# Eight modulation products moved from the recurrent input to layer 1's MLP norm

## The reference, cut to what matters

```
ml = silu(c) @ w_mod[i] + b_mod[i]        # six parts of 1024, for each layer i
mc = silu(c_ctx) @ w_mod[i] + b_mod[i]
hl = modulate(rmsnorm(xl, g_pre_mix[i]), ml[0], ml[1])
xl_new = xl + ml[2] * rmsnorm(y_l, g_post_mix[i])
h2 = modulate(rmsnorm(xl_new, g_pre_mlp[i]), ml[3], ml[4])
xl_new = xl_new + ml[5] * rmsnorm(sqrelu_mlp(h2, ...), g_post_mlp[i])
```

## Time and profile before

| | us |
|---|---|
| median of 3 runs | 1718.69 |
| profiled execution | 1716.11 |
| its span | 1714.3 |
| TensorE busy | 1612.4 (94%) |
| VectorE busy | 1153.9 (67%) |
| ScalarE busy | 552.9 (32%) |
| GpSimd busy | 337.2 (20%) |

### The profile page before, as it was taken

How to read it: one execution, slowest core, us unless ns; L and a number is a source line. 1 busy time by engine, 2 the same in 40 slices (tenths; PEclk the granted TensorE clock), 3 DMA queues, 4 the chain that set the end, 5 groups by cost and what they waited for, 6 DMA issues and landing times.

```text
span 1714.3 us, 26801 instructions
## 1 busy us (share of the span) xinstructions
PE 1612.4 (94%) x10898; PEld 1409.1 (82%) x10898; DVE 1153.9 (67%) x1649; ACT 552.9 (32%) x1111; POOL 337.2 (20%) x300
## 2 busy tenths in 40 slices
PE   7998889999999999999888999999999988889997
PEld 6887779998888999987546588888888874779997
DVE  6855777777687788769764574444444788577776
ACT  5434141112724122153575430202022465541112
POOL 1100333332032333300000121111111100133331
PEclk9999999999999999999999999999999998999999
DMA  7733655556755555532101532222222231224551
GB/s 299 260 121 125 254 213 174 184 183 229 262 183 201 181 184 184 189 147 104 52 1 50 203 117 87 97 100 86 98 98 87 74 136 37 79 102 172 185 185 51
DMA packets 69940, 247.54 MB, mean 144 GB/s; under 512 B 7504, under 2 KB 10576, under 8 KB 69712
## 3 DMA queue, kind: packets, MB, share of 16 engines
q1 hardware_dynamic: 69840, 246.18, 40.5%
HBM read 245.10 MB, written 1.05 MB: 144 GB/s over the span
## 4 chain that ended last, share of the span: by engine, by line
PE 71%; DVE 15%; issue 8%; ACT 5%; DMA 1%; POOL 0%; SPq 0%; DVEq 0%; ACTq 0%; POOLq 0%
PE psum L373 19%; PE psum L375 19%; PE psum L374 19%; DVE lo_ring L334 4%; PE psum L1120 2%; PE psum L388 1%; PE psum L390 1%; PE psum L389 1%; DVE c_soft L2152 1%; ACT c_p L1939 1%; DVE relu L1388 1%; PE psum L488 1%; DVE c_conf L2046 1%; DVE c_p L2160 1%; DVE hid_lo L1389 1%
## 5 line engine op out<-in xcount | busy, mean ns | idle before, releaser
L2321 POOL TENSOR_SCALAR hi_ring<-raw_ring 128x1024 fp32r<-128x1024 f32 x296 | 337.0, 1140 | 1355.5 <-PE psum L375 963.5
L334 DVE TENSOR_TENSOR lo_ring<-raw_ring,hi_ring 128x1024 fp32r<-128x1024 f32 x348 | 507.2, 1459 | 51.3 <-PE psum L375 20.9
L373 PE MATMUL psum<-x_hi,hi_ring 128*128 128x256 f32 (+1 forms) x1464 | 460.9, 315 | 16.3 <-DVE x_lo L879 10.5
L374 PE MATMUL psum<-x_lo,hi_ring 128*128 128x256 f32 (+1 forms) x1464 | 456.1, 312 | 0.0
L375 PE MATMUL psum<-x_hi,lo_ring 128*128 128x256 f32 (+1 forms) x1464 | 456.0, 311 | 0.0
L373 PEld LDWEIGHTS psum<-x_hi,hi_ring 128*128 128x128 f32 x1464 | 281.0, 192 | 38.8 <-issue 16.9
L373 PE MATMUL psum<-hid_hi,hi_ring 128*128 128x256 f32 (+1 forms) x992 | 304.8, 307 | 6.4 <-DVE hid_lo L1389 6.4
L375 PE MATMUL psum<-hid_hi,lo_ring 128*128 128x256 f32 (+1 forms) x992 | 302.9, 305 | 0.0
L374 PE MATMUL psum<-hid_lo,hi_ring 128*128 128x256 f32 (+1 forms) x992 | 302.3, 305 | 0.0
L374 PEld LDWEIGHTS psum<-x_lo,hi_ring 128*128 128x128 f32 x1464 | 281.1, 192 | 14.9 <-issue 0.2
L375 PEld LDWEIGHTS psum<-x_hi,lo_ring 128*128 128x128 f32 x1464 | 281.0, 192 | 14.7
(11 more groups left out here) (424 smaller groups left out, 1996.1 us busy)
## 6 DMA issues: line engine op xcount, KB each, us to landing
raw_ring<-weights SPq DMA_DIRECT2D x460, 512.0 KB, 3.2
h_const<-hyb_consts SPq DMA_DIRECT2D x1, 1088.0 KB, 11.1
x<-xT SPq DMA_DIRECT2D x1, 1024.0 KB, 7.5
x<-ctxT SPq DMA_DIRECT2D x1, 1024.0 KB, 16.3
outT<-x SPq DMA_DIRECT2D x4, 256.0 KB, 2.5
shared<-shared_consts SPq DMA_DIRECT2D x1, 398.0 KB, 13.0
par<-params SPq DMA_DIRECT2D x1, 301.5 KB, 7.6
```

Source lines behind the costliest of these rows:

```text
L334: nc.vector.tensor_tensor(lo_ring[:, s, :], raw_ring[:, UNIT_AT[u] % RAW_SLOTS, :], hi_ring[:, s, :].bitcast(F32), ALU.subtract).then_inc( ...
L373: nc.tensor.matmul(bank(u % BANKS, T), w_hi, hi[:, k, 0:T], start=(k == 0), stop=False)
L374: nc.tensor.matmul(bank(u % BANKS, T), w_hi, lo[:, k, 0:T], start=False, stop=False)
L2321: nc.gpsimd.tensor_scalar(hi_ring[:, n % SPLIT_SLOTS, :], raw_ring[:, slot, :], 1.0, 0.0, ALU.mult, ALU.add).then_inc(hi_ready, 1)
```

## The change

The eight products of the recurrent input go; those of the gates stay. All later products thereby stand eight items of `w_mod` earlier in their order, and the last eight get a new place, "gate_mlp", in layer 1 between the two sums of squares. In the stream they stand behind the MLP's first three units. The batches are cut anew, six instead of five; the last one is copied out by ScalarE behind layer 1's squares, turned by TensorE after the first quarter of layer 1's MLP, and taken by VectorE in the second, with the sixth coefficient part alone; the other five parts are worked out in layer 0's MLP as before.

```diff
-REC_MODS = {j: 3 if j == 2 else 1 for j in range(REC_FIRST - 1, KT)}
+REC_MODS = {j: 0 for j in range(REC_FIRST - 1, KT)}
...
-_STREAM += [MLP_UNITS - LEAD, ("mean3", 2), EARLY, ("pre_mix", 7), L2_UNITS - EARLY - MLP_UNITS + LEAD, ("post_mix", 8), ("post_sum", 6), MLP_UNITS - LEAD, L2_UNITS]
+_STREAM += [MLP_UNITS - LEAD, ("mean3", 2), EARLY, ("pre_mix", 7), L2_UNITS - EARLY - MLP_UNITS + LEAD, ("post_mix", 8), ("post_sum", 6), MLP_UNITS - LEAD, L2_UNITS - MLP_UNITS + LEAD, ("gate_mlp", 8), MLP_UNITS - LEAD]
...
-BATCHES = [10, 10, 14, 7, 7]
+BATCHES = [10, 10, 10, 7, 7, 4]
...
-    SUMS_TAKEN = [0, 2, 4, 5]
+    SUMS_TAKEN = [0, 2, 4, 5, 6]
...
-        if late:
-            turn_batch(pe, 4)
+        if m > 1:
+            turn_batch(pe, m + 2)
...
                 take_sums(dve, 2)
-                coef_dve(dve, link, 1)
+                coef_dve(dve, link, 1, 0, 5)
+            if m == 3 and i == 1:
+                take_sums(dve, 3)
+                coef_dve(dve, link, 1, 5)
...
-                squares_act(act, L.norm + 2, L.T, x, "x_updated", L.updated)
+                squares_act(act, L.norm + 2, L.T, x, "x_updated", L.updated, "gate_mlp" if L.l else None)
...
-                if L.l == 0:
-                    mods(pe, "post_mix")
+                mods(pe, "gate_mlp" if L.l else "post_mix")
```

## The result

The kernel after takes 1726.03 us (median of 20 runs, 1719.79 to 1736.31), the kernel before on the same chip 1720.81 (20 runs, 1717.72 to 1725.52): ratio 1.0032 [1.0023, 1.004]. The forecast was 1718.8 with a range of 1714.0 to 1723.0: the time lies outside. The profiled execution of after is its fastest run, 1719.79 us with a span of 1718.0, 3.7 us longer than the 1714.3 of before.

What follows compares the result with a forecast made beforehand. TensorE was suspected, with VectorE and ScalarE next limiting the recurrent stage. Recurrent +0.2 and layer 1 -1.1 + 0.2 + 0.4 + 0.4 made 0.1 us more: median 1718.8 us, range 1714.0 to 1723.0.

Steps and rivals of the forecast that it cites:

- Small parts: Layer 1's row copy, extra turning, coefficient steps and the new batch cut: 0.4 us for the turning, nothing for the rest.
- D: Rival, chance 0.03: the change doesn't do what it says, for instance a batch waits for its rows; a few tenths of us.
- VectorE and ScalarE take over in the recurrent stage: Recurrent stage: gate 2 waits for ScalarE's read behind VectorE's last taps; 1.2 us of 5.2 gained, new idle 3.7 us.
- Rival A: Chance 0.09: TensorE carries the recurrent stage after all and the whole 5.2 us is won, 1713.4 us.
- The clock behind the idle: Recurrent stage: TensorE's clock falls after the new idle before gate 2, costing 1.4 us, so the stage ends 0.2 later.
- rival B: Chance 0.24: VectorE and ScalarE take over as said, but the clock does not fall in front of gate 2; 1717.4 us.
- Layer 1's norm: Post-mix norm: products fill TensorE's 3.04 us idle at full clock, 1.1 us gained, less 0.2 (weights) and 0.4 (GpSimd).
- late weights: Layer 1's post-mix norm: the last product's weights arrive at 1505.7, so the sums end at 1509.8; 0.2 us taken.
- The collision with GpSimd: Layer 1: the fourth MLP unit's hi half on GpSimd runs beside VectorE's gating and slows it; 0.4 us, bounds 0 and 0.85.
- rival C: Chance 0.16: layer 1's products go on the path, their last weights landing 2 us later; +2.3 us, 1721.0.
- The copy of the rows: Layer 1: ScalarE's copy of the product rows, 0.42 us, is hidden before the rstd's wait for the sums: nothing.
- The turning: Layer 1's MLP: one more turning on TensorE, 0.51 us busy, some overlapping the next matmul; 0.4 us more.

Runs made afterwards that it cites:

- E10: Kernel before with the region of y and the hidden tiles 192 bytes later (hid at distance 0, as in after), no product moved: 1724.46 us, ratio 1.0032.
- E11: Kernel after, unedited, run again on the same chip: 1722.79 us, ratio 1.0022 against the kernel before.
- E1: Kernel after with y and the hidden tiles put back at their old addresses (distance 64): 1718.78 us, ratio 1.0004 against the kernel before.
- E8: Kernel after with x and hid both at distance 192: 1713.61 us, ratio 0.9966 against the kernel before.
- E12: Kernel after with x at distance 64, hid at 0 for 512 columns and 192 for 256: 1704.64 us, ratio 0.9932 against the kernel before.
- E5: Kernel before with x and hid both at distance 192, lam's place moved in front of x_hi: 1709.35 us, ratio 0.9945.
- E9: Kernel before with x at distance 64, hid at 0 for 512 columns and at 192 for 256: 1707.54 us, ratio 0.9935.
- E6: Kernel before with x at distance 32 and hid at 96, a single run: 1728.02 us.
- E3: Kernel before with everything 64 bytes further, weights too, so all distances kept: 1717.47 us, ratio 0.999.
- E4: Kernel before with x_hi and what follows moved 64 bytes, y and hid 64 more (x at distance 64, hid at 192): 1710.59 us, ratio 0.9948.
- E2: Kernel before with y and the hidden tiles 64 bytes further (hid at distance 128): 1724.23 us, ratio 1.0028.
- E7: Kernel before with x at distance 160 and hid at 224, a single run: 1730.7 us.

## Why the prediction was wrong

**The step that failed** is the last sentence of "Small parts": "The new cut of the batches (10, 10, 10, 7, 7, 4) ends each batch at the place where it ended before, at most 20 columns instead of 28: nothing." I priced the cut by what it computes. It also sizes two tiles, these push hid_hi by 320 bytes, and the 2304 matmuls of 256 columns on it each lose 0.0022 us, while the 672 of 512 columns gain 0.0023: +3.5 us by the rows (+3.9 with the last 192), +3.3 to +7.7 by E10's interval. No rival had it either; D looked for the batches' side effects in waits. Of the 7.2 us above the forecast 2.1 are the kernel before itself, whose median is 1720.81 over 20 runs and was 1718.69 over the first 3.

**VectorE and ScalarE take over in the recurrent stage: right.** Gate 2 waits for ScalarE's r_i, the idle is 3.44 us (forecast 3.7), 1.08 us is won (forecast 1.2). Rival A, the whole 5.2 us, is refuted by those rows.

**The clock behind the idle: right in direction, too cheap.** I took 1.4 us. It fell in four of five executions and then cost 1.4 to 2.6 (5.03 to 6.19 against 3.60); in the profiled execution of after it cost nothing, which is rival B. The Trainium skill ("TensorE: Matmul & The Clock Gate", "Part 1: The HAM clock gate") has half rate as the resting state; these four agree, at 0.56 in E11's stretch. From the end of the first units to the start of the output units the stage takes 63.83 us before and 62.76 after, 1.1 less; in E1, E11, E8 and E12 it takes 64.22, 65.31, 64.24 and 64.50, against 63.83, 63.92, 63.19 and 63.99 in the kernels with the products in place (before, E10, E5, E9), so 0.4 to 1.4 more. The forecast was 0.2 more.

**Layer 1's norm: right in sum, not in its parts.** Forecast -1.1 + 0.2 + 0.4 = -0.5; measured -0.69, with the clock at 1.00 as expected. The -1.1 shrank to -0.7 since the sums ended 0.88 us behind the last square (1512.48), where I took 0.45 for the four matmuls left. Of the 0.2 for late weights nothing shows. The collision with GpSimd, the 0.4 in it, had no occasion: the weights of that unit came later than I took, and its hi half ran when VectorE's gating was nearly done:

```profile
1511.61 1.05 POOL L2324 TENSOR_SCALAR hi_ring<-raw_ring 128x1024 fp32r<-128x1024 f32 x1 [8.80 <-DMA raw_ring<-weights]
```

VectorE's last gating instruction ran from 1511.03 to 1511.72, in 0.69 us like the others. The products ended at 1508.58, 3.59 us behind the sum before them, where the forecast had 3.7 to 4.8; no DMA stands in front of them, so rival C did not happen.

**Small parts.** The copy of the rows was hidden, in front of a stat read that ends its wait at the sums, as forecast:

```profile
1512.38 0.36 ACT L509 ACTIVATE mod_rows<-psum 128x256 f32<-128x256 f32 x1
1513.39 0.47 ACT L1128 ACTIVATE stat<-psum,eps 128x256 f32<-128x256 f32 x1 [0.65 <-PE psum L1120]
```

The turning cost 0.36 of the 0.4 us taken:

```profile
1567.90 0.51 PE L469 MATMUL psum<-shared,mod_rows 128*128 128x8 f32 x4
```

**The sum.** By rows: gates -1.1, norm -0.7, turning +0.4, pace +3.9 make +2.5 of the profiles' +3.7. Most of the rest lies in falls of the clock that sit elsewhere in each execution. From one matmul to the same one in the other trace, after gains 3.1 us in the first 30 us and 1.2 between 1534 and 1554 (times of before), and loses 1.6 between 885 and 905, 1.6 between 967 and 987, 1.8 between 1329 and 1349 and 0.9 between 1369 and 1390: +1.6 together, at each place with a fall in one of the two traces that the other lacks or has shorter; -0.4 is left in small steps. Two of these places:

```profile
20.00:40.00 20.00, 20.00 (x148) 18.91 (x148) 12.90 (x39) 12.47 (x22) 0.00 (x0) 0.83 0.65 239
1340.00:1360.00 20.00, 19.94 (x93) 17.60 (x94) 12.94 (x30) 11.36 (x25) 3.35 (x3) 1.00 0.29 103
```

Those are of before; of after:

```profile
20.00:40.00 20.00, 20.00 (x174) 18.36 (x174) 15.78 (x45) 13.52 (x24) 0.00 (x0) 1.00 0.81 286
1340.00:1360.00 20.00, 18.72 (x79) 16.22 (x80) 11.02 (x24) 12.09 (x27) 3.40 (x3) 0.91 0.25 79
```

One such fall is worth up to 1.8 to 3.4 us (0.09 and 0.17 of 20 us), as much as the steps of this change, so two single profiles can't be subtracted whole; the repeated runs carry the verdict. By them the moved products are worth +0.0004 (E1 against before), -0.0010 (E11 against E10), -0.0003 (E12 against E9) and +0.0021 (E8 against E5) of the time, all inside their intervals: the forecast's +0.1 us for them is not refuted, and nothing finer is shown. The change's 5.2 us of medians (1726.03 - 1720.81) are near what the rows give for an execution in which the clock falls at the new idle: +3.9 for the pace, +0.4 to +1.4 for the stage, -0.7 and +0.4, so 4.0 to 5.0.

## What to carry to other kernels

Ask of every changed constant which tiles it sizes and what is allocated behind them; on a kernel bound by TensorE, compare the start-to-start pace of matmuls that the change doesn't touch, before any stage that it does. When a time moves by a few tenths of a per cent, shift the addresses alone in the old kernel (E10) before explaining the change. And work taken from an engine is worth only what the next one leaves: one cycle of VectorE, read to its end, gave the 1.1 us of 5.2 ahead of time.

## What the runs showed of the hardware

In these runs the pace of back-to-back split-float matmuls goes with the distance, modulo 256 bytes, between the moving tile and the weights' tile. Start to start within a unit, us, at the clock's upper level, without a wait:

```
distance   256 columns        512 columns   seen on
0          0.1200             0.2267        x (before, after), hid (after, E10)
32         0.1167             0.2333        x (E6)
64         0.1178 (0.1133)    0.2288        hid (before, E1, E3), x (E4, E9, E12)
96         0.1200             0.2333        hid (E6)
128        0.1187             0.2333        hid (E2)
160        0.1175             0.2342        x (E7)
192        0.1133 or 0.1178   0.2333        hid (E4: 0.1133), both (E5, E8)
224        0.1183             0.2333        hid (E7)
```

The 0.1133 in brackets is what a few units at distance 64 took (E3, E4, E12, and one in E9). Distances to other tiles don't order these paces: hid_hi stands 128 bytes from x_hi in E2 and in E4, with 0.1187 and 0.1133. The best distance for one width is not that for the other, which is why E9 keeps two places. The spread is 6% of a matmul at 256 columns and 3% at 512. The lo tiles have the same distances as the hi tiles here, so which of the pairs matters was not separated; nor was the cause found (the loads of weights run beside the matmuls and read the other tile, but no run isolates them), nor what switches distances 64 and 192 between their paces within a run. The Trainium skill ("TensorE: Matmul & The Clock Gate", "Wait — 56ns, not 53.3ns?") gives the pace at full clock as columns by 2.4 GHz plus about 2.5 ns, by estimate 109 and 216 ns here; every pace above is slower than that and not one number, so for these matmuls the measurement decides.
